# Conditioning weights in chunks of 128 rows by 2048 columns, and products of constants while TensorE waits

## The reference

```python
for l in range(DEPTH):                                      # DEPTH = 2, D_MODEL = 1024
    mod = jax.nn.silu(c) @ ada_w[l] + ada_b[l]              # c: 1 prompt row, 8 sample rows; ada_w[l]: 1024 x 6144
    sh1, sc1, g1, sh2, sc2, g2 = split(mod, 6)
    h = _layernorm(x) * (1.0 + sc1) + sh1
    proj = h @ w_in[l]                                      # 1024 x 3592
    ...                                                     # heads A: differential softmax attention (paged past of
    ...                                                     # 1024 keys for the samples); heads B: gated DeltaNet
    mix = concat([o_a, o_b]) @ w_out[l]
    x = _layernorm(ALPHA * x + g1 * mix) * ln1_g[l] + ln1_b[l]
    h2 = _layernorm(x) * (1.0 + sc2) + sh2
    f = _swiglu(h2, ...) if l % 2 == 0 else _moe_swiglu(h2, ...)   # dense; top 2 of 8 experts
    x = _layernorm(ALPHA * x + g2 * f) * ln2_g[l] + ln2_b[l]
```

## Time and profile before

| | us |
|---|---|
| median of 3 runs | 2557.95 (2556.85 to 2568.91) |
| the profiled execution | 2563.26 |
| its span (first to last instruction) | 2561.6 |
| TensorE busy in it | 2233.8 (87%) |
| start, until the first projection | 91.1 |
| layer 0, mixer of tokens, until 580.7; its output projection, norms, dense mixer | 938 |
| layer 1, mixer of tokens, until 1468.4; experts until | 2529 |

### The profile page before, as it was taken

How to read it: one execution, slowest core, us unless ns; L and a number is a source line. 1 busy time by engine, 2 the same in 40 slices (tenths; PEclk the granted TensorE clock), 3 DMA queues, 4 the chain that set the end, 5 groups by cost and what they waited for, 6 DMA issues and landing times.

```text
span 2561.6 us, 35629 instructions
## 1 busy us (share of the span) xinstructions
PE 2233.8 (87%) x14217; PEld 1603.7 (63%) x14218; DVE 478.4 (19%) x1155; ACT 413.4 (16%) x864; POOL 89.1 (3%) x165
## 2 busy tenths in 40 slices
PE   6998876778999999978767787999799998989996
PEld 3675554765677666655557656994499647836743
DVE  1043212532100021441134332000100000000002
ACT  1123442111100011234421121000000001001002
POOL 0000230000000000002300000000000000000000
PEclk8799896958999999988968597999899999998998
DMA  9644884013233332367810105877477776996992
GB/s 302 185 130 131 280 305 133 1 38 115 83 129 113 119 101 82 115 200 254 300 43 1 53 17 182 293 259 302 151 259 273 285 267 251 390 400 225 370 381 80
DMA packets 260562, 486.44 MB, mean 190 GB/s; under 512 B 15072, under 2 KB 143788, under 8 KB 260370
## 3 DMA queue, kind: packets, MB, share of 16 engines
q1 hardware_dynamic: 246578, 437.10, 49.3%
q0 software_dynamic: 13792, 46.74, 5.4%
HBM read 474.81 MB, written 8.98 MB: 189 GB/s over the span
## 4 chain that ended last, share of the span: by engine, by line
PE 76%; DMA 8%; DVE 6%; ACT 4%; issue 4%; SPq 1%; POOL 0%; POOLq 0%; DVEq 0%; ACTq 0%
PE ps L713 19%; PE ps L789 16%; PE ps L856 9%; PE ps L755 4%; DMA region<-in_cache_k_dram 3%; PE ps L826 3%; PE ps L900 2%; PE ps L769 2%; PE ps L876 2%; PE ps L999 2%; PE ps L697 2%; PE ps L951 2%; DMA ring<-in_moe_w_down_dram 2%; PE ps L702 1%; PE ps L1080 1%
## 5 line engine op out<-in xcount | busy, mean ns | idle before, releaser
L789 PE MATMUL ps<-region,ring 128*128 128x224 f32 (+1 forms) x2816 | 435.8, 315 | 6.1 <-DMA ring<-in_moe_w_up_dram 6.1
L789 PEld LDWEIGHTS ps<-region,ring 128*128 128x128 f32 x2816 | 423.7, 191 | 26.4 <-issue 24.0
L713 PE MATMUL ps<-hT,ring 128*128 128x320 f32 x1472 | 403.5, 438 | 6.1 <-ACT hT L1381 6.1
L713 PEld LDWEIGHTS ps<-hT,ring 128*128 128x128 f32 x1472 | 283.2, 193 | 125.5 <-ACT hT L1381 6.6
L856 PE MATMUL ps<-ring,big 128*128 128x512 f32 (+1 forms) x528 | 234.7, 600 | 6.1 <-DMA ring<-in_moe_w_down_dram 6.1
L856 PEld LDWEIGHTS ps<-ring,big 128*128 128x128 f32 (+1 forms) x528 | 94.2, 182 | 138.3 <-issue 128.0
L1080 PE MATMUL ps<-C,region 128*128 128x128 f32 x512 | 92.4, 312 | 33.1 <-DMA region<-in_cache_k_dram 31.3
L2142 DVE TENSOR_TENSOR big<-hT,ps 128x896 f32<-128x896 f32 (+3 forms) x24 | 19.8, 827 | 484.6 <-PE ps L789 484.6
L658 POOL DMA_DIRECT2D region<-in_cache_k_dram x128 | 70.4, 550 | 967.3 <-PE ps L1080 929.9
L1080 PEld LDWEIGHTS ps<-C,region 128*128 128x128 f32 x512 | 61.3, 155 | 61.8 <-DMA region<-in_cache_k_dram 47.6
L755 PE MATMUL ps<-big,ring 128*128 128x320 f32 x352 | 95.0, 433 | 1.0 <-DVE big L2116 1.0
(11 more groups left out here) (341 smaller groups left out, 2104.8 us busy)
## 6 DMA issues: line engine op xcount, KB each, us to landing
ring<-in_moe_w_up_dram SPq DMA_DIRECT2D x144, 1024.0 KB, 8.0
ring<-in_moe_w_down_dram SPq DMA_DIRECT2D x80, 1024.0 KB, 9.3
ring<-in_ada_w_dram SPq DMA_DIRECT2D x48, 1024.0 KB, 8.1
region<-in_cache_k_dram POOLq DMA_DIRECT2D x128, 256.0 KB, 4.5
region<-in_cache_v_dram SPq DMA_DIRECT2D x128, 256.0 KB, 4.7
ring<-in_w_in_dram SPq DMA_DIRECT2D x28, 1024.0 KB, 5.5
ring<-in_moe_w_up_dram SPq DMA_DIRECT2D x32, 768.0 KB, 5.6
ring<-in_dense_w_up_dram SPq DMA_DIRECT2D x22, 1024.0 KB, 5.1
```

What stands on the lines that cost most here:

```text
L713: m = mm(ps[:, b + o, 0:n], w[:, k, o * P:(o + 1) * P], rhs[:, k, 0:n], start=(first and k == 0), stop=(last and k == nk - 1))
L789: m = mm(ps[:, 2 * part + t // 2, 256 * (t % 2):256 * (t % 2) + n], w[:, kk, t * P:(t + 1) * P], XE[:, k, t0:t0 + n], start=(k == 0 and t ...
```

## The change

It has three parts. **Chunks**: a conditioning chunk is now 128 rows by 2048 columns, 8 KB in one piece per partition. Its `ada_rows` is four products of 512 columns, one in each column group, with the same 32 columns of `siluC`; eight chunks in a row accumulate in one bank and give a third of `mod` of a layer. For each third there is one copy (`mod_rows`), one `ada_turn` of four products, and two `mod_add`. The start does the first third of layer 0 alone (8 chunks), with `ln(0)` after the second. The first third of layer 1 moves to layer 0's attention norm and DeltaNet stage; six of its chunks are loaded ahead of the V pages, two behind them, and `w_out` of layer 0 comes after these. The prompt attention keeps 16 chunks, two a unit, with one turn in the fifth unit and one behind the last. **Start**: ScalarE issues the first six chunks itself; 13 of the small loads are counted in a semaphore of their own, which is waited for later, before the first layer norm on ScalarE and VectorE; the history's turn goes ahead of `h_ready`. **Fills**: `fill(n, b)` issues n products of constants (`onesm` by `mean1`, 128 by 128 by 128) into a bank that nothing uses then, ahead of a wait of TensorE.

```diff
-ADA_EARLY = 2 * D // CH
-ADA_LATE = 4 * D // CH
+ADA_W = 2 * D
+ADA_LATE = 2 * KT
...
-N_VO = 6 + ADA_LATE
+N_VO = [6 + ADA_LATE + KT, 6 + ADA_LATE]
...
-POS_WIN = [2 * ADA_EARLY, 2 * ADA_EARLY + N_WIN + N_VO + MLP_POS]
+POS_WIN = [KT, KT + N_WIN + N_VO[0] + MLP_POS]
...
-POS_MLP = [p + N_VO for p in POS_VO]
+POS_MLP = [p + n for p, n in zip(POS_VO, N_VO)]
 POS_ADA = [p + 2 for p in POS_VO]
-POS_WO = [p + 2 + ADA_LATE for p in POS_VO]
+POS_NEXT = POS_ADA[0] + ADA_LATE
+POS_WO = [p - 4 for p in POS_MLP]
...
+        def ada_pos(l, q, k):
+
+            if q == 0:
+                return k if l == 0 else POS_NEXT + k
+            return POS_ADA[l] + KT * (q - 1) + k
+
+        def ada_src(l, q, k):
+            return ada_w[l][k * P:(k + 1) * P, ADA_W * q:ADA_W * (q + 1)]
...
-            if half == 0 and not gate:
-                return s_modev, ADA_EARLY * (l + 1)
-            return s_modev, 2 * ADA_EARLY + ADA_LATE * l + (4 if half == 0 else 16 if gate else 12)
+            return s_modev, 2 * (3 * l + (2 if half else 1 if gate else 0) + 1)
...
+            def ld_late(dst, src):
+                N_TAB[1] += 16
+                sp.dma_start(dst, src).then_inc(s_tab2, 16)
...
+            ld_late(dP[:], t_dp.rearrange("p (a n) -> p a n", a=2))
+            ld_late(dS[:], t_ds)
...
+        N_TABLES, N_LATE = 16 * 13, 16 * 13
...
+            for k in range(RING, KT):
+                load_ada(0, 0, k)
...
+                for q in (1, 2):
+                    for k in range(KT):
+                        load_ada(l, q, k)
+
+                def out_weights():
+                    for c in range(4):
+                        load(chunk(POS_WO[l] + c), wsrc(w_out[l], CH * c), POS_WO[l] + c)
+
+                if l == 0:
+                    for k in range(RING):
+                        load_ada(1, 0, k)
+                else:
+                    out_weights()
...
                 if l == 0:
+                    for k in range(RING, KT):
+                        load_ada(1, 0, k)
+                    out_weights()
                     mlp(dw_up[0], dw_dn[0], POS_MLP[0])
...
+            def fill(n, b):
+
+                for _ in range(n):
+                    mm(ps[:, b, 0:P], onesm[:], mean1[:], start=True, stop=True)
...
             def h_ready(m):
+                fill(14, 3)
                 pe.wait_ge(s_h, KT * (m + 1))
                 pe.wait_ge(s_hs, m + 1)
...
+            def ada_rows(l, q, k, bank):
+                pos = ada_pos(l, q, k)
+                pe.wait_ge(*full(pos))
+                for g in range(4):
+                    m = mm(ps[32 * g:32 * g + 32, bank, :], siluC[:, k, :], ring[:, pos % RING, 512 * g:512 * (g + 1)],
+                           start=(k == 0), stop=(k == KT - 1))
                 m.then_inc(s_chunk, 1)
...
+            def ada_turn(l, q, bank):
+                pe.wait_ge(s_adE, 3 * l + q + 1)
+                out = ps[:, bank, 0:144].rearrange("p (g t j) -> p g t j", g=4, t=4)
+                for t in range(4):
+                    m = mm(out[:, :, t, :], mrow[:, t * P:(t + 1) * P],
+                           ident.rearrange("p (g j) -> p g j", g=4)[:, :, 0:9], start=True, stop=True)
                 m.then_inc(s_adT, 1)
...
+            for k in range(KT):
+                ada_rows(0, 0, k, 6)
+                if k == 1:
                     ln(0)
...
+            ada_turn(0, 0, 5)
...
-                h_ready(2 * l)
-
                 pe.wait_ge(s_hist, 16 * (l + 1))
                 for f in range(12):
                     m = tr(ps[:, 7, 24 * f:24 * f + 24], rowb[0:24, f * P:(f + 1) * P], ident[0:24, 0:24])
                 m.then_inc(s_histT, 1)
+                if l == 0:
+                    pe.wait_ge(s_tab2, N_LATE)
+                    pe.wait_ge(s_modev, 2)
+                h_ready(2 * l)
...
+                    if b == 3:
+                        fill(2, 3)
...
                     if u == 0:
+                        fill(8, 3)
...
-                    n = 2 * ADA_EARLY + ADA_LATE * l + 2 * u
-                    ada_rows(n, 6, 0, n)
-                    ada_rows(n + 1, 6, CH, 0)
+                    for k in range(2 * (u % 4), 2 * (u % 4) + 2):
+                        ada_rows(l, 1 + u // 4, k, 6 + u // 4)
...
-                    ada_turn(n, 7, 0, n)
-                    ada_turn(n + 1, 7, 32, 0)
+                    if u % 4 == 0 and u:
+                        ada_turn(l, 1, 6)
+                ada_turn(l, 2, 7)
...
-                pe.wait_ge(s_modev, 2 * ADA_EARLY + ADA_LATE * (l + 1))
...
+                    if isinstance(i, int) and i == 0:
+                        pe.wait_ge(*mods(l, 1))
...
+                def next_rows(ks):
+                    if l == 0:
+                        for k in ks:
+                            ada_rows(1, 0, k, 7)
+
                 for h in range(H):
+                    next_rows(((), (), (0,), (1, 2))[h])
+                    if l:
+                        fill((0, 2, 6, 8)[h], 7)
                     pe.wait_ge(s_oq, H * l + h + 1)
...
+                next_rows((3, 4, 5))
+                fill(6 if l == 0 else 20, 2)
...
+                            if T == 2:
+                                fill(2 if v else 9, 1 if v else 7)
+                            elif v == 0 and x == 1:
+                                if l == 0:
+                                    pe.wait_ge(s_adE, 4)
+                                fill(16, 7)
...
+                            if T == 2:
+                                fill(1, 1)
...
+                    spare = 0 if smp else 6
                     if smp:
+                        fill(4, spare)
...
+                        fill(3, spare)
...
+                    if l == 0 and T == 0:
+                        ada_turn(1, 0, 0)
+                    fill(4 if smp or (l == 0 and T == 0) else 7, spare)
...
+                    fill(2, spare)
...
+                    fill(2, spare)
...
+                    if not smp:
+                        fill(4, spare)
...
+                next_rows((6, 7))
+                fill(8 if l == 0 else 20, 6)
...
+                fill(14, 6)
...
+                fill(10, 0)
...
+            for k in range(RING):
+                pos = ada_pos(0, 0, k)
+                nc.scalar.dma_start(ring[:, pos % RING, :], ada_src(0, 0, k)).then_inc(full(pos)[0], 16)
...
+            def mod_rows(l, q, bank):
+                act.wait_ge(s_chunk, ada_pos(l, q, KT - 1) + 1)
+                if l or q:
+                    act.wait_ge(s_adT, 3 * l + q)
+                A(mrow, ps[:, bank, :], ACT.Copy).then_inc(s_adE, 1)
+
+            act.wait_ge(s_tab2, N_LATE)
+            ln_stats(0)
...
+                if l == 0:
+                    mod_rows(0, 0, 6)
...
-                    n = 2 * ADA_EARLY + ADA_LATE * l + 2 * u
-                    mod_rows(n, 6, 0)
-                    mod_rows(n + 1, 6, CH)
+                    if u == 4:
+                        mod_rows(l, 1, 6)
+                    if u == 7:
+                        mod_rows(l, 2, 7)
...
+                if l == 0:
+                    mod_rows(1, 0, 7)
...
+            def mod_add(l, q, bank):
+                dve.wait_ge(s_adT, 3 * l + q + 1)
+                for h in range(2):
+                    f = 16 * q + 8 * h
+                    V.scalar_tensor_tensor(out=mod[:, l, f:f + 8, :], in0=ps[:, bank, 72 * h:72 * h + 72].rearrange("p (f j) -> p f j", j=9),
+                                           scalar=1.0 if (q, h) in ((0, 1), (2, 0)) else 0.0,
+                                           in1=vecT[:, 0, 48 * l + f:48 * l + f + 8].rearrange("p (f o) -> p f o", o=1).to_broadcast([P, 8, 9]),
+                                           op0=ALU.add, op1=ALU.add).then_inc(s_modev, 1)
+
+            dve.wait_ge(s_tab2, N_LATE)
+            ln(0)
...
+                if l == 0:
+                    mod_add(0, 0, 5)
...
-                    n = 2 * ADA_EARLY + ADA_LATE * l + 2 * uu
-                    if uu > 0:
-                        mod_add(n - 2, 7, 0)
-                        mod_add(n - 1, 7, 32)
+                    if uu == 5:
+                        mod_add(l, 1, 6)
                     p_probs(uu)
-                mod_add(n, 7, 0)
-                mod_add(n + 1, 7, 32)
+                mod_add(l, 2, 7)
...
+                if l == 0:
+                    mod_add(1, 0, 0)
```

## The result

The changed kernel takes **2483.06 us** (median, 2481.15 to 2489.09), the kernel before 2558.98 beside it: a ratio of 0.970, 95% interval 0.968 to 0.972. The prediction said 2475, 2448 to 2522. The profiled execution has a span of 2481.1 us against 2561.6, and a mean granted clock of 0.952 against 0.907. Its total is 2482.7; the sum of the prediction had 2480.6 for that execution.

A forecast was written before the change was run, and what follows sets the result against it. TensorE near full clock bounds two thirds of the span, untouched; gains come from the start, waits and low-clock attention and DeltaNet stages. 34.7 + 9 + 18 - 4 + 25 = 82.7 off, giving 2475 us at the median, range 2448 to 2522.

The forecast's parts named there:

- Start: Until the first projection: tables land at 22 us, eight chunks remain, projection at 56.4 for 91.1; gain 34.7, from 27 to 44.
- Waits ahead of projections: Fourteen constant products fill each wait for h, so projections start warm; with layer 1's history turn, gain 9.
- Prompt attention: Both layers: one turn in four units and warm first chunk rows, if DMA keeps up; gain 18, 9 a layer.
- 3 us a layer: Prompt attention: at 349 GB/s DMA would end last, by about this much.
- Sample attention: K pages wait on DMA behind the chunks' backlog, six chunks queued for four of w_out; loss 4, 0 to 10.
- DeltaNet: DeltaNet stages of both layers: clock gain 34 less 9 for moved chunks and fills; gain 25, from 5 to 40.
- The gain of the clock: DeltaNet stretches: full clock takes off 68, two thirds (45) on the path, three quarters of that believed: 34.
- The price of the norm: Attention's norm: moved chunks and fills exceed the gaps by 4 in layer 0, 4.6 in layer 1; 9 in both.
- the early chunks only move: Rival: chunks and tables crowd, moved chunks fall on DeltaNet's path, clock doesn't hold; within 0.5% (2545 to 2571); chance 0.03.
- The cold one: Rival: the clock doesn't hold in the DeltaNet stretches and fills are paid cold; 2532 us; chance 0.14.
- the slower one: Rival: TensorE becomes the late engine in latency-bound stages, some 345 fills cold without gaps; about 2672 us; chance 0.03.
- The warm one: Rival: everything warm and tables early, 45 for 34, 9 more at the start, 4 not lost; 2451 us; chance 0.14.

The follow-up runs named there:

- kernel 4: Changed kernel with the first six chunks issued by SyncE behind the 13 tables, ahead of the 13 late ones, none by ScalarE: 2479.81 us.
- kernel 5: Changed kernel with one wait more: ScalarE issues its six chunks only when the first 13 tables have landed: 2475.97 us.
- kernel 6: As kernel 4, with ScalarE's and VectorE's waits for the late tables moved behind the first layer norm: 2473.45 us.
- Kernel 2: Changed kernel with only the fourteen constant products ahead of each wait for h, no other fills: 2515.66 us.
- kernel 1: Changed kernel without any constant products, the chunks and the start alone: 2526.76 us.
- kernel 7: Changed kernel with each conditioning chunk loaded by two DMAs in pieces of 1 KB: 2486.05 us.
- kernel 10: Changed kernel with all eight chunks of layer 1's first third loaded behind layer 0's V pages, w_out after them: 2481.15 us.
- kernel 12: kernel 11 with all eight chunks of layer 1's first third also loaded behind layer 0's V pages: 2465.2 us.
- kernel 3: Kernel before the change with constant products alone, ahead of each wait for h, in the norm (few) and the DeltaNet stage: 2515.83 us.
- kernel 8: Changed kernel with fewer constant products in layer 1's attention norm (1, 1, 1 for 2, 6, 8) and behind the norm (0 and 4 for 6 and 20): 2477.72 us.
- kernel 9: Changed kernel with 17 constant products for 9 ahead of the sample levels, and 3 ahead of each head's state products but the first: 2481.21 us.
- kernel 11: Changed kernel with the edits of kernel 6 and kernel 8, and 17 constant products for 9 ahead of the sample levels: 2465.05 us.

## Why the prediction was right, step by step

**The sum.** It is 2.1 us off (82.7 against 80.5) with single terms off by 2 to 6.5, which cancel: the start 3.9, the prompt attention 6.5 and the DeltaNet stage 2.0 too high; the sample attention 4.4 and the rest 6.0 too low. That the mechanisms are there the runs show; that the total came so close is in part luck.

**Start, 34.7 predicted, 30.8 measured.** The steps behind the first product held: 8.3 of turning, chunks of 1.07 taken and 0.89 measured, 34.2 us in all where the sum had 34.4. The step that failed is the landing of the tables: bounds of 10 and 24, 22 taken, 26.16 measured, outside both. The mechanism and the rate were right (402 GB/s for 409): by 24.00 us 863 of the 864 packets of ScalarE's chunks had moved, so x_sample came behind all of them. The upper bound counted too few bytes and too fast an end: SyncE's queue had moved 2.88 MB by 26.16, not 2.4, as late tables share it, and in the last 2 us (24.00 to 26.20) the rate was 246. Kernels 4 to 6 show that it is the order. The Trainium skill's "DMA: Bandwidth & Descriptors", section "Issuing engines are not separate DMA queues", says that such loads interleave and only issue time is saved. The rows agree that they interleave (831 and 833 packets, 402 GB/s together); that section doesn't say what share of the bytes each queue gets, and that set the landing here.

**Waits ahead of projections, 9 predicted, 9 found, and 6 without a term.** From the kernel before to the changed one the stretches from projection to scores are 1.9 and 2.1 us shorter and the dense mixer's first matrix 2.5 (193.2 to 190.7), where 2.2 was taken for each; the router's product takes 1.28 for 2.36, 1.1 as said; the history's turn is 1.4. Kernel 2 against kernel 1 gives 11.1 by the medians and 2.4, 3.1 and 2.8 by the marks of the three stretches with a large projection (of the 3.1 only 1.1 lie in the dense mixer's first matrix). The stretch with the router is 3.3 shorter as well, but not by this term: the router's product takes 2.36 in both, and kernel 1's profiled execution stands for 20.80 us ahead of the experts' first product, where every other trace has 14.8 to 15.4. Besides, each output projection (x128) went from 37.6 (kernels 1 and 2) to 34.6: the ten constant products ahead of it make it start at full clock, 3 us a layer that the prediction had in no term.

**Prompt attention, 18 predicted, 11.5 measured.** The turns: in the middle units stand 4.2 to 4.7 us apart where 4.3 was said; the first step takes 5.9 and 6.5, and the steps around a turn or at half clock 4.8 to 6.0. The two mis-sized pieces: the warm first rows took 1.92 as said, but TensorE then waited 2.39 us for VectorE, so their 1.6 are hidden (kernel 1, without a constant product, has 39.2 and 41.2 us for the stretch, the changed kernel 39.9 and 41.1); and the clock still falls once in each layer's stretch, with two chunks' rows at 3.20 and 3.64.

```profile
204.65 1.92 PE L971 MATMUL ps<-ring,siluC 128*32 128x512 f32 x16
208.96 0.33 PE L1076 MATMUL ps<-C,region 128*128 128x128 f32 x1 [2.39 <-DVE region L1976]
```

DMA didn't end last, as said, and at 415 GB/s against the 349 of the earlier trace rows it is the length of the pieces (kernel 7). At 349 it would not have ended last either: that "3 us a layer" was wrong by kernel 7, and didn't follow from its own terms (ten chunks at 3.0 are 30 us, and the last pair is used at 30). The Trainium skill's 358 GB/s for a core ("DMA: Bandwidth & Descriptors", "Specifications") is no limit here; on one core alone 415 were moved.

**Sample attention, a loss of 4 predicted, a gain of 0.4 measured.** +2.1 in layer 0, -2.5 in layer 1, whose queue the change doesn't alter. Kernels 10 and 12 show that the mechanism is there: six chunks ahead of the V pages cost 6 us of this stage, and behind the V pages 3.5 in the norm instead. But the step was wrong in what it compared: the kernel before has four w_out chunks in that place, and with this old order layer 0's stage takes 134.2 and, in kernel 3, 136.7, against 135.4 to 137.4 with the new one. Two chunks more make no clear difference in these traces.

**DeltaNet, 25 predicted, 23 measured.** The gain of the clock was to be 34; the stages are 34.8 shorter (15.8 and 19.0), with the chunks that layer 0's took on. Of this 28.7 belong to the constant products, as kernel 1 has 154.8 and 155.8; the other 6 come without them, and are partly how profiled executions differ (layer 1's stage with the same products takes 159.8, 155.8 and 157.0 in the kernel before and kernels 1 and 2). The clock is 0.89 and 0.90, not near 1 as the prediction asked for. The price of the norm was to be 9, and is 11.8: the constants were sized right (20 products took 4.63, 0.23 each), but the first sums and products of the norm still run at half clock, the second sum in 1.27 (x2) where the prediction had it warm at 0.70. By kernel 8 this price bought nothing behind it. (The 14 constants ahead of the third preparation were said to fit when warm; by the prediction's own 3.4 us against 2.95 they don't, by 0.4.) That the samples' levels stay at half clock for a gap of 1.92 us was in no step; the prediction had only a general deduction for fills that don't cover a wait, a quarter of 45.

**The rivals.** That the early chunks only move falls by the ratio, 0.970. The cold one (2532) and the slower one (2672) fall: all constant products together took 97.4 us for 345, 0.28 each, near the warm 0.24. The warm one (2451) has its place in kernels 6 and 9: tables early gave 9.6 by the medians, warm levels are 8.8 for both layers by the marks, but little of that reached the median (2 us in kernel 9). With the early tables and the warm levels in one kernel, and fewer constants in the norm besides, kernel 11 stands at 2465, not 2451.

## What to carry to other kernels

Constant products ahead of a wait pay when the work behind it is long and clock-bound, and cost when they are longer than the wait: read each gap, put in just what closes it, and look at the gaps that are left, for constants in one of 1.92 us gave 3.3 to 4.6 us of the steps behind it. Then follow this to the end of the stage: in five of six places the state products that came next ran at half clock, and much of the gain was gone. When a second queue is given large loads at the start, the small loads that the first product waits for must have landed, or be issued ahead of them in the same queue, for two queues took turns by packets and not by bytes; moving a wait later is the other half of it. After each such edit ask what is late next; here it was a wait for tables that nothing needed yet, and then the last chunk.

## What was not expected of the hardware

- Small loads of one queue beside 6 MB of another: the last of 13 landed at 26.16 us with the other's pieces at 8 KB, at 17.11 with 1 KB and a lower rate of the whole (340 for 402 GB/s), and at 12.3 to 13.4 with the large loads behind them (12.0 to 13.4 with kernels 11 and 12).
- TensorE, busy 15.97 of 16 us, was granted 0.51 in layer 0's state products (515 to 531 us), and, busy 6.08 of 8 us, 1.00 just ahead of the samples' levels (482.4 to 490.4). The Trainium skill ("TensorE: Matmul & The Clock Gate", section "What's actually happening") says that activity releases the throttle; busy time in the profile is not that activity, by these rows.
- The same eight state products of a head (x16) took 3.78 and 2.05 us in the two layers of one execution (kernel 9).
